# An encoder block's FFN: the down product as seven block products on one core

## Reference

```python
hn = rmsnorm(h, norm_ffn_g[l])
gate, up = jnp.split(hn @ w_ffn_up[l], 2, axis=-1)
gate = dwconv(gate, conv_ffn_w[l], conv_ffn_b[l], left=FFN_CONV // 2)
h = h + (jax.nn.silu(gate) * up) @ w_ffn_down[l]
return h[:, N_META:]
```

## Time and profile before

| | us |
|---|---|
| median of 3 runs | 1365.32 |
| the runs | 1353.3, 1365.32, 1365.39 |
| span of the profiled execution (its own time; another execution than the three) | 1355.8 |
| one turn of the loop over groups, mean of nine | 61.36 |
| PE busy in such a turn | 61.36 |
| DVE, ACT, POOL busy in such a turn | 42.92, 20.86, 5.21 |

### The profile page before, as it was taken

How to read it: one execution, slowest core, us unless ns; L and a number is a source line. 1 busy time by engine, 2 the same in 40 slices (tenths; PEclk the granted TensorE clock), 3 DMA queues, 4 the chain that set the end, 5 groups by cost and what they waited for, 6 DMA issues and landing times.

```text
span 1355.8 us, 17820 instructions
## 1 busy us (share of the span) xinstructions
PE 1304.5 (96%) x6218; PEld 1045.2 (77%) x6218; DVE 956.6 (71%) x1452; ACT 629.6 (46%) x959; POOL 138.1 (10%) x108
## 2 busy tenths in 40 slices
PE   5999998799999999999899999999999999999998
PEld 5999997466666666687678888888888888888886
DVE  5687559777777776577878656777777766667755
ACT  6486824367777776534444233333324242333320
POOL 0000033300000001232201010110101010110101
PEclk9999899699999999999999999999999999999999
DMA  6011200000000014110021211121112112121103
GB/s 212 32 51 40 71 0 1 1 1 9 9 9 10 9 40 164 57 37 9 15 83 50 61 40 63 38 70 31 62 31 70 39 60 64 39 70 31 62 31 124
DMA packets 30569, 64.27 MB, mean 47 GB/s; under 512 B 6483, under 2 KB 7187, under 8 KB 30517
## 3 DMA queue, kind: packets, MB, share of 16 engines
q1 hardware_dynamic: 30516, 63.57, 14.5%
HBM read 59.20 MB, written 4.23 MB: 47 GB/s over the span
## 4 chain that ended last, share of the span: by engine, by line
PE 84%; DVE 7%; ACT 5%; issue 2%; POOL 1%; DMA 1%; SPq 0%; DVEq 0%; POOLq 0%; ACTq 0%
PE banks L2547 31%; PE banks L100 11%; PE banks L102 11%; PE banks L101 11%; PE banks L1914 2%; PE banks L1829 2%; PE banks L1915 2%; PE banks L1934 2%; PE banks L1916 2%; PE banks L1937 2%; PE banks L1935 2%; ACT e_f L1468 1%; DVE lam_t L1611 1%; PE banks L1793 1%; PE banks L856 1%
## 5 line engine op out<-in xcount | busy, mean ns | idle before, releaser
L2547 PE MATMUL banks<-x_hi,slot_h 128*128 128x512 f32 x616 | 245.0, 398 | 4.3 <-ACT gate L2220 3.1
L2547 PE MATMUL banks<-x_hi,slot_l 128*128 128x512 f32 x616 | 243.8, 396 | 0.0
L2547 PE MATMUL banks<-x_lo,slot_h 128*128 128x512 f32 x616 | 243.7, 396 | 0.0
L2321 DVE TENSOR_TENSOR slot_l<-up_raw,slot_h 128x512 fp32r<-128x512 f32 x127 | 101.1, 796 | 149.9 <-ACT slot_h L2178 149.1
L2178 ACT ACTIVATE slot_h<-up_raw 128x512 fp32r<-128x512 f32 x127 | 79.7, 627 | 169.7 <-PE banks L2547 169.7
L2547 PEld LDWEIGHTS banks<-x_hi,slot_h 128*128 128x128 f32 x616 | 116.0, 188 | 35.5 <-issue 3.8
L100 PE MATMUL banks<-dn_h,a_h 128*128 128x512 f32 x352 | 137.8, 392 | 2.3 <-issue 2.3
L101 PE MATMUL banks<-dn_l,a_h 128*128 128x512 f32 x352 | 137.5, 391 | 0.0
L102 PE MATMUL banks<-dn_h,a_l 128*128 128x512 f32 x352 | 137.4, 390 | 0.0
L2547 PEld LDWEIGHTS banks<-x_hi,slot_l 128*128 128x128 f32 x616 | 116.0, 188 | 26.8
L2547 PEld LDWEIGHTS banks<-x_lo,slot_h 128*128 128x128 f32 x616 | 116.0, 188 | 26.5
(11 more groups left out here) (311 smaller groups left out, 2564.8 us busy)
## 6 DMA issues: line engine op xcount, KB each, us to landing
up_raw<-in_w_up SPq DMA_DIRECT2D x88, 256.0 KB, 2.7
dn_raw<-in_w_down SPq DMA_DIRECT2D x22, 512.0 KB, 4.2
win_raw<-in_w_in SPq DMA_DIRECT2D x11, 512.0 KB, 3.2
x_tm<-in_x_tm SPq DMA_DIRECT2D x8, 512.0 KB, 4.3
wo_raw<-in_w_out SPq DMA_DIRECT2D x16, 256.0 KB, 4.0
h<-in_x_tm SPq DMA_DIRECT2D x8, 512.0 KB, 5.8
out<-h SPq DMA_DIRECT2D x16, 256.0 KB, 2.0
sum_recip<-recip SPq DMA_DIRECT2D x8, 256.0 KB, 3.5
```

Source lines behind the costliest of these rows:

```text
L2321: nc.vector.tensor_tensor(s_l[slot], x, f32(s_h[slot]), ALU.subtract).then_inc(sem["up_lo"], 1)
L2547: ins = nc.tensor.matmul(o, s[slot][:, k], xs[w], start=fresh and k == 0 and n == 0, stop=k == 3 and n == 2, skip_group_check=not fresh)
```

## The change

The 256x1024 by 1024-token down product of a group becomes seven block products too. The activations are split into 2 x 2 blocks (tile of D_FF, half of the tokens), the weights into 2 x 2 blocks (tile of D_FF, half of the columns). Product k (`down(g, k)`) multiplies one sum of activation blocks by one sum of weight blocks into banks 4 to 7: four token tiles, three matmuls each. DVE makes eight block sums in place (`sum_a1` to `sum_b4`). ACT makes the 14 high parts of a group and DVE the 14 low parts, in two slots for each operand. Products 0, 4 and 5 start the banks afresh; the others add onto what is there. After products 1 and 6 DVE adds the four banks onto columns 512 to 1023 of the first 512 tokens of h. After products 0, 2, 3, 4 and 5 ACT copies the banks into one of three staging buffers in two pieces of 128x1024 (`stage`), which lie where h was, and POOL issues an accumulating DMA of 512 KB for each piece onto the output in DRAM (`add_out`). For that SP stores h to the output ahead of unit (0, 1)'s loads. PE runs one product of the previous group behind every second gate/up product; the last group's seven follow alone (`down_alone`). POOL's low parts go. Two semaphores are dropped elsewhere. In the diff below the removed lines of the old units on ACT and DVE are left out.

```diff
-        dn_raw.append(place(f"dn_raw{e}", at, (D,))); at += D
-        a_h.append(place(f"a_h{e}", at, (SEQ,), F32R)); at += SEQ
-        a_l.append(place(f"a_l{e}", at, (SEQ,), F32R)); at += SEQ
+    base = at
+    av = [place(f"act{e}", base + 2 * D + 4 * D * e, (SEQ,)) for e in range(2)]
+    b_raw = [place(f"dn_raw{e}", base + D * e, (D,)) for e in range(2)]
+    a_slots = [[place(f"a_{n}{b}", base + 3 * D + HALF_D * (2 * b + m), (HALF_D,), F32R) for m, n in enumerate("hl")]
+               for b in range(2)]
+    b_slots = [[place(f"dn_{n}{b}", base + (5 * D, 7 * D)[b] + HALF_D * m, (HALF_D,), F32R) for m, n in enumerate("hl")]
+               for b in range(2)]
+    at += 8 * D
+    s2_a = place("act_sum", con["late"] + 8 + 2 * P, (HALF_D,))
...
-        return NU * g + n + 1
+    SUM_A3, SUM_B3, SUM_A2, SUM_A1, SUM_B2, SUM_A4, SUM_B1, SUM_B4 = range(1, 9)
+    ADDED_BY_DVE = {1: 0, 6: 4}
+    STAGED = {0: 0, 2: 1, 3: 2, 4: 3, 5: 4}
+    STAGE_OF = {0: 2, 2: 0, 3: 1, 4: 2, 5: 0}
+    FRESH = (0, 4, 5)
+    def down_sums(g, n):
+        return 8 * g + n
+    def down_splits(g, k, b=1):
+        return 14 * g + 2 * k + 1 + b
+    def down_done(g, k, i=3):
+        return ND * g + 4 * k + i + 1
+    def down_added(g, k, i=3):
+        return 4 + 8 * g + ADDED_BY_DVE[k] + i + 1
+    def down_staged(g, k, p=1):
+        return 10 * g + 2 * STAGED[k] + p + 1
+    def stage_uses(g, k):
+        return g if k == 3 else 2 * g + (k in (4, 5))
+    def a_of(k):
+        return (part(av, "11"), s2_a, part(av, "12"), part(av, "22"), part(av, "21"), part(av, "11"), s2_a)[k]
+    def b_block(e, c):
+        return b_raw[e][:, HALF_D * c:HALF_D * c + HALF_D]
+    def b_of(k):
+        return (b_block(0, 0), b_block(0, 0), b_block(0, 1), b_block(0, 0), b_block(1, 0), b_block(0, 1), b_block(1, 1))[k]
...
             load(2 * g + a, A12)
         def load_down(g):
-            ready(sp, "dn_mm", NU * g)
+            ready(sp, "dn_lo", 14 * g)
             for e in range(2):
-                sp.dma_start(dn_raw[e], dram["w_down"].rearrange("(t p) n -> t p n", p=P)[bass.ds(2 * g + e, 1)]
+                sp.dma_start(b_raw[e], dram["w_down"].rearrange("(t p) n -> t p n", p=P)[bass.ds(2 * g + e, 1)]
                              .rearrange("o p n -> p (o n)")).then_inc(sem["dn_in"][e], 16)
+        sp.wait_ge(sem["hn"], NT)
+        for i in range(XT):
+            cols = slice(0, HALF_D if i < 4 else D)
+            sp.dma_start(out[P * i:P * i + P, cols], h[:, i, cols]).then_inc(sem["stored"], 16)
         load_unit(0, 1)
         with sp.Fori(1, GROUPS) as g:
             load_unit(g, 0)
...
-            sp.dma_start(out[P * i:P * i + P, 512 * c:512 * c + 512], h[:, i, 512 * c:512 * c + 512])\
-              .then_inc(sem["stored"], 16)
-        sp.wait_ge(sem["stored"], 16 * NU)
+        for i in range(4):
+            sp.wait_ge(sem["dn_read"], down_added(GROUPS - 1, 6, i))
+            sp.dma_start(out[P * i:P * i + P, HALF_D:D], h[:, i, HALF_D:D]).then_inc(sem["stored"], 16)
+        sp.wait_ge(sem["stored"], 16 * (XT + 4))
...
-        def low_down(g):
-            for e in range(2):
-                pool.wait_ge(sem["dn_hi"], 2 * g + e + 1)
-                nc.gpsimd.tensor_tensor(dn_l[e], dn_raw[e], f32(dn_h[e]), ALU.subtract).then_inc(sem["dn_lo"], 1)
-        with pool.Fori(0, GROUPS) as g:
-            low_down(g)
+        def add_out(g, k):
+            rows, c = {0: (0, 0), 2: (4, 1), 3: (4, 0), 4: (0, 0), 5: (4, 1)}[k]
+            b = STAGE_OF[k]
+            for p in range(2):
+                r = P * (rows + 2 * p)
+                pool.wait_ge(sem["dn_act"], down_staged(g, k, p))
+                nc.gpsimd.dma_start(out[r:r + 2 * P, HALF_D * c:HALF_D * c + HALF_D].rearrange("(i p) n -> p i n", p=P),
+                                    staged[b][:, 2 * p:2 * p + 2, :], accum_op=ALU.add).then_inc(sem["added"][b], 16)
+        for g in range(GROUPS):
+            for k in STAGED:
+                add_out(g, k)
+        for b in range(3):
...
+        def high_a(g, k):
+            if k == 0:
+                ready(act, "dn_mm", down_done(g - 1, 6))
+                act.wait_ge(sem["prod"], 4 * g + 1)
+            if k >= 2:
+                act.wait_ge(sem["dn_mm"], down_done(g, k - 2))
+            if k in (3, 4):
+                act.wait_ge(sem["prod"], 4 * g + {3: 2, 4: 4}[k])
+            if k in (1, 2, 5, 6):
+                act.wait_ge(sem["dn_sum"], down_sums(g, {1: SUM_A2, 2: SUM_A3, 5: SUM_A1, 6: SUM_A4}[k]))
+            nc.scalar.activation(a_slots[k % 2][0], a_of(k), ACT.Copy).then_inc(sem["dn_hi"], 1)
+        def high_b(g, k):
+            if k in (0, 4, 6):
+                act.wait_ge(sem["dn_in"][0 if k == 0 else 1], 16 * g + 16)
+            else:
+                act.wait_ge(sem["dn_sum"], down_sums(g, {1: SUM_B2, 2: SUM_B3, 3: SUM_B4, 5: SUM_B1}[k]))
+            nc.scalar.activation(b_slots[k % 2][0], b_of(k), ACT.Copy).then_inc(sem["dn_hi"], 1)
+        def high_down(g, k):
+            high_a(g, k)
+            high_b(g, k)
+        def stage(g, k, p):
+            b = STAGE_OF[k]
+            if p == 0:
+                uses = stage_uses(g, k)
+                if not isinstance(uses, int) or uses > 0:
+                    act.wait_ge(sem["added"][b], 32 * uses)
+            act.wait_ge(sem["dn_mm"], down_done(g, k, 2 * p + 1))
+            nc.scalar.activation(staged[b][:, 2 * p:2 * p + 2, :], bank(4 + 2 * p, 2).rearrange("p (i n) -> p i n", i=2),
+                                 ACT.Copy).then_inc(sem["dn_act"], 1)
         def tap(g, m):
             ready(act, "acc_dve", dve_reads(g, 0, E12))
             if m == 0:
-                ready(act, "a_lo", 4 * g)
+                ready(act, "prod", 4 * g)
                 act.wait_ge(sem["halo_mm"], g + 1)
                 for e in range(2):
...
-            if a and isinstance(g, int) and g == 0:
+        def unit_0(g, d=None):
+            if d is not None:
+                high_down(d, 0)
+            high_s3(g, 0)
+            ready(act, "prod", 4 * g)
+            read(g, 0, P1, 0, "11")
+            if d is not None:
+                high_a(d, 1)
+            read(g, 0, P5, 1, "22")
+            if d is not None:
+                stage(d, 0, 0)
+                stage(d, 0, 1)
+                high_b(d, 1)
+                high_down(d, 2)
+            high_a22(g, 0)
+            read(g, 0, P6, 2, "12")
+            high_s4(g, 0)
+            if d is not None:
+                high_down(d, 3)
+            high_a11(g, 1)
+            high_s1(g, 1)
+            high_a12(g, 1)
+            if d is not None:
+                stage(d, 2, 0)
+                stage(d, 2, 1)
+            tap(g, 0)
+            read(g, 0, P4, 6, "21")
+            high_s2(g, 1)
+            tap(g, 1)
+            if d is not None:
+                high_down(d, 4)
+                silu(g, 0)
...
+        def unit_1(g, d=None, more=True):
+            high_s3(g, 1)
+            if d is not None:
+                silu(g, 1)
+                act.wait_ge(sem["conv2"], 2 * g + 2)
+            read(g, 1, P1, 0, "11")
+            if d is not None:
+                high_down(d, 5)
+                stage(d, 3, 0)
+                stage(d, 3, 1)
+            read(g, 1, P5, 1, "22")
+            if d is None:
                 silu(g, 0)
                 silu(g, 1)
+            high_a22(g, 1)
+            read(g, 1, P6, 2, "12")
+            if d is not None:
+                stage(d, 4, 0)
+                stage(d, 4, 1)
+                high_down(d, 6)
+            high_s4(g, 1)
             if more:
+                high_a11(g + 1, 0)
+            if d is not None:
+                stage(d, 5, 0)
+                stage(d, 5, 1)
             if more:
+                high_s1(g + 1, 0)
+                high_a12(g + 1, 0)
+                high_s2(g + 1, 0)
...
+        def down_alone(g):
+            high_down(g, 0)
+            high_down(g, 1)
+            for k in range(7):
+                if k in STAGED:
+                    stage(g, k, 0)
+                if k < 5:
+                    high_down(g, k + 2)
+                if k in STAGED:
+                    stage(g, k, 1)
         high_s2(0, 0)
...
+        def low_down(g, k):
+            low_a(g, k)
+            low_b(g, k)
+        def down_sum(o, x, y, op):
+            nc.vector.tensor_tensor(o, x, y, op).then_inc(sem["dn_sum"], 1)
...
+        def sum_a3(g):
+            dve.wait_ge(sem["prod"], 4 * g + 3)
+            down_sum(part(av, "12"), part(av, "11"), part(av, "12"), ALU.subtract)
+        def sum_b3(g):
+            for e in range(2):
+                dve.wait_ge(sem["dn_in"][e], 16 * g + 16)
+            down_sum(b_block(0, 1), b_block(1, 1), b_block(0, 1), ALU.subtract)
+        def sum_a2(g):
+            dve.wait_ge(sem["dn_sum"], down_sums(g, SUM_A3))
+            down_sum(s2_a, part(av, "22"), part(av, "12"), ALU.subtract)
+        def sum_a1(g):
```

(191 more changed lines are left out.)

150 lines of the change are left out of this document (18 added, 132 removed).

## The result

The changed kernel takes 1423.58 us by median (1421.07 to 1432.55, 4 runs) against 1360.86 (1353.3 to 1365.39, 4 runs): ratio 1.0484, 95% interval 1.0424 to 1.0543, slower. The page of the profile after, in the order: busy time, PE's busy share in 40 slices, the granted clock, the DMA engines' share, the two queues, one group of DMA issues.

The account below looks back on a forecast made before the run. TensorE was taken as the bound: -27.2 for ten groups, 0 for cover, +0.5 start, +8.2 tail make -18.5 us, from the median 1365.3 to 1347. The range was 1331 to 1368.

Parts of the forecast that it names:

- The group of 58.64 us: One turn of the FFN loop: 12 fewer down matmuls at 0.227 us, 58.64 in place of 61.36 us, PE-bound.
- the cover that was 0.7 us thin: Second unit's third product waits for ACT's read: 10.4 of 11.1 us used, cost 0, bounds 0 to 0.7 per group.
- the distances of 6.6 and 3.8 us: Tail: 6.6 us of DVE work after the last gate/up product, then 3.8 us between product ends for D3 to D5.
- 27.2 + 2.72: Middle: ten groups' down products save 27.2 us; 2.72 is group 9's D6, run after the last gate/up product.
- The start: Before the FFN: storing h first may delay unit (0,1)'s loads; +0.5 us, bounds -0.5 to +2.
- It becomes the bound at (58.64 - 10) / 10 = 4.9 us, three copies' time: Accumulating DMAs in each group: they bind from 4.9 us of engine time each; 3.3 us, two copies' time, was taken.
- latency alone is harmless: Staging buffers: each is reused 22 us or later after its last eviction, so DMA latency costs nothing.
- 5.9 us as the price per issue: POOL's ten issues per group: between 0 and 5.9 us each they only delay the transfer's start.
- +4.9: Tail: four accumulating DMAs of 3.3 us queued, the last ending about 8 us behind PE; bounds 0 to +12.
- the accumulating DMAs that bind: Rival at staging-buffer reuse and weight loads: binds from 4.9 us per DMA, kernel just over 1380 to 1515 us; chance 0.12.
- Case 1: Rival in each group: the cover on ACT and DVE leaks 0.7 to 2.5 us, giving 1354 to 1372; chance 0.20.
- case 2: Rival in each group: accumulating DMAs bind at staging-buffer reuse, from 4.9 us per DMA, slower side; chance 0.12.

Follow-up runs that it names:

- e4_none: The changed kernel with no DMA from GpSimd and no wait on one, five of seven products not reaching the output: 1342.41 us.
- e2_ring: The changed kernel with 1536 bytes per partition for GpSimd's DMA descriptors in place of 1024, SBUF tiles 512 bytes higher: 1354.54 us.
- e1_pieces: The changed kernel with each accumulating DMA of 512 KB issued as two of 256 KB: 1364.61 us.
- e3_plain: The changed kernel with the same 110 DMAs as plain writes, without accumulation, so sums in the output are left out: 1339.18 us.
- e7_dve3_ring: The changed kernel with product 3 also added by DVE, 8 accumulating DMAs per group, two staging buffers and 1536 descriptor bytes: 1350.65 us.
- e8_merge_ring: e7_dve3_ring with DVE adding the last group's products 4 and 5 onto staged products 0 and 2, four DMAs at the end: 1344.54 us.

## Why the prediction was wrong

The forecast was 1347, in a range of 1331 to 1368, with 0.62 on faster.

**Right: PE, ACT and DVE.** The group of 58.64 us, DVE at 48 and ACT at 34.5, the cover that was 0.7 us thin and held, the distances of 6.6 and 3.8 us at the end. DVE measured 47.9 and ACT 34.2. By e4_none the middle gave 30.0 us for the forecast's 27.2 + 2.72. The start cost nothing that the table shows, for a forecast of 0.5.

**The step that failed** is "It becomes the bound at (58.64 - 10) / 10 = 4.9 us, three copies' time", with "latency alone is harmless". The estimate of the engines' time came out: 3.3 us forecast, 3.66 in the changed kernel and 3.33 in e2_ring. That was in part luck: it was two copies of 1.6 us, and it is 2.4 plain writes of 1.36. But I took the time that the engines are busy with a DMA for the distance from one DMA to the next, as if any number could be under way. One was. The distance is the time from issue to landing and 0.3 more, 6.1 us, and the bound is 58.64 / 10 = 5.86 us per DMA. It is exceeded by 0.26 us at the least, 2.5 us per group, and by the mean of 6.28 us by 0.42, 4.2 us per group. The text had the number in hand: it gave 5.9 us as the price per issue at which POOL fills a group, and took it for a far bound.

From there the loss can be added up. The queue alone gives the length of the kernel: first issue at 729.35, 109 intervals with a mean of 6.31 us, 6.6 from the last issue to the end of the span, 1423.3. In the 87 intervals of 6.28 us POOL falls behind by some 36 us. Of these 28.1 show as longer middle (660.2 for 632.1): ACT waits for staging buffers, and PE behind it. The rest went into the slack of the buffers' reuse, which puts the first large stall off to the fourth group, and into the backlog; that split was not measured. When the last gate/up matmul starts, at 1332.3, 14 DMAs are still to be issued (12 in e2_ring at that point): 5.1 us to the first, 13 x 6.11 to the last, 6.6 from there to the end of the span, which makes the 91.0 measured.

**The end** was the second term of the wrong size: "+4.9" for the queue behind PE. With room for two it is 56.7 - 34.3 = 22.4 us (e2_ring), in the changed kernel 91.0 - 34.3 = 56.7. Even without a loss in the middle, then, the kernel would not have been faster than before (e2_ring, ratio 0.9987): the drained queue takes back what the products save. Ten DMAs at 4.3 to 5.4 us do not fit behind seven products at 3.8; I had counted four at 3.3.

**The rivals.** The slower side was there as the accumulating DMAs that bind, with 0.12, and the place was right: reuse of a staging buffer, issues on POOL. Its condition was wrong, three to four copies' time on the engines; two and a half and a wait for room were enough. Case 1, a leak of the cover, did not happen. The range left case 2 out, with 1380 as its least time, because its condition was priced by bandwidth alone.

The page "Collectives: The Full Stack" of the Trainium skill (The bandwidth ceiling) had given 1.93 copies for a reducing transfer between cores; here, into the core's own DRAM, it is 2.4 plain writes (3.33 to 1.36). The page "DMA: Bandwidth & Descriptors" of the Trainium skill (SWDGE vs HWDGE vs iDMA) says that the descriptors of DMAs issued from GpSimd lie in rings in an area of SBUF. The runs agree as far as they can: with 64 bytes more of that area in each partition, two are under way for one.

## What to carry to other kernels

A DMA's price is two numbers, the engines' time and the distance at which the next may start; a queue that must keep up is judged by the second, and an operation that no row shows has no second number until it is run. Where GpSimd issues DMAs, ask first how many fit into the room that the kernel leaves for their descriptors: 64 bytes more gave back 67 us here. Work handed to a queue also has to be drained at the end, so the last turn of a loop wants its own, shorter way out.

## What the runs showed of the hardware that I had not expected

- The room for descriptors of GpSimd's DMAs limits how many are under way. The most at any issue, by the landings in the traces: with 1024 bytes one of 512 KB (in 110, 88 and 84 DMAs) or three of 256 KB, with 1088 two of 512 KB, with 1536 two of 512 KB or five of 256 KB. In descriptors of 16 bytes (64, 68, 96) that bounds an accumulating DMA of 256 rows of 2 KB to 33 or 34 and one of 128 rows to 17, 18 or 19, if the whole area can be used and nothing else holds an issue back. Two per row and one more is the least count that fits; it was worked out, not seen. That 64 bytes change one at a time into two was measured.
- The count does not say when the next one starts. With 1088 and 1536 bytes a third DMA of 512 KB never starts before both of a pair have landed. In e1_pieces, with work waiting, three go together, a fourth when the first of them has landed (1303.44, landing 1303.19), and the next three only when that fourth has (1308.57, landing 1308.21). The reason stays open; it is why the drained end stays at 4.3 to 5.4 us per DMA.
- An accumulating DMA of 512 KB keeps POOL for 1.22 us and the 16 DMA engines for 3.3 to 3.7 (changed kernel, e2_ring), a plain one for 0.73 and 1.36 (e3_plain). With no other one under way it lands 5.8 us after the start of its issue (median); the plain ones, up to three at a time, after 3.3 and 3.5.
- The same instructions ahead of the FFN had different granted clocks in different executions. In the stretch from 500 to 600 us it was 1.00 in the profiled execution of before and 0.90 in that of the changed kernel, and the FFN began at 664.4 and 672.1:

```profile
500.00:600.00 100.00, 96.45 (x466) 72.07 (x465) 63.10 (x91) 55.25 (x80) 22.97 (x18) 1.00 0.28 96
```

```profile
500.00:600.00 100.00, 96.92 (x425) 71.74 (x424) 57.54 (x83) 52.27 (x74) 20.50 (x16) 0.90 0.28 95
```

The other two profiles whose FFN begins at 672 (e7_dve3_ring, e8_merge_ring) have 0.90 there too, the ten that begin at 660 to 666 have 0.98 or 1.00. What decides it was not looked into.
